# A hybrid decoder layer on one core: the recurrent gates' block products as two row tiles of 64

## The reference

```python
LRU_WIDTH = 512; LRU_BLOCKS = 8; LRU_BLOCK = 64

def rglru_group(u, gate_in, conv_w, conv_b, w_gate_a, b_gate_a, w_gate_x, b_gate_x, lru_lambda):
    xc = causal_conv_of_width_4(u) + conv_b
    xb = xc.reshape(B, T, LRU_BLOCKS, LRU_BLOCK)
    r = sigmoid(einsum("bthi,hij->bthj", xb, w_gate_a).reshape(B, T, C) + b_gate_a)
    i = sigmoid(einsum("bthi,hij->bthj", xb, w_gate_x).reshape(B, T, C) + b_gate_x)
    log_a = -8.0 * r * softplus(-lru_lambda)
    a, b = exp(log_a), sqrt(-expm1(2.0 * log_a)) * (i * xc)
    hseq = associative_scan(h[t] = a[t] * h[t - 1] + b[t])
    return hseq * gelu(gate_in)

# the layer
h   = x + RMSNorm( [ rglru_group ; diff_attn_group ] W_out )
out = h + RMSNorm( relu(RMSNorm(h) W_up)^2 W_down )
```

## Time and profile before

| | |
|---|---|
| time, median of 3 runs | 1154.75 us (1152.32 to 1155.97) |
| time of the profiled execution | 1152.76 us |
| span of the profiled execution, first to last instruction | 1151.0 us |
| busy TensorE, share of the span | 1122.8 us, 98% |
| busy VectorE | 785.3 us, 68% |
| busy ScalarE | 399.2 us, 35% |
| mean granted TensorE clock | 0.996 |

### The profile page before, as it was taken

How to read it: one execution, slowest core, us unless ns; L and a number is a source line. 1 busy time by engine, 2 the same in 40 slices (tenths; PEclk the granted TensorE clock), 3 DMA queues, 4 the chain that set the end, 5 groups by cost and what they waited for, 6 DMA issues and landing times.

```text
span 1151.0 us, 14008 instructions
## 1 busy us (share of the span) xinstructions
PE 1122.8 (98%) x5110; PEld 908.4 (79%) x5110; DVE 785.3 (68%) x1127; ACT 399.2 (35%) x728; POOL 52.7 (5%) x94
## 2 busy tenths in 40 slices
PE   7999999999989999999999999999999999999996
PEld 6888887777756788878888888888888888888885
DVE  6666765756577546888867667766766666766768
ACT  7433933545567326642212112212221211211222
POOL 0300001000121110000000000000000000000010
PEclk9999999999999999999999999999999999999998
DMA  6111323111010456111121011110211102111062
GB/s 229 56 37 36 136 84 89 58 37 38 21 35 19 148 182 200 73 37 74 37 73 36 36 73 36 45 64 36 73 36 41 69 36 73 36 36 73 37 234 113
DMA packets 23397, 83.11 MB, mean 72 GB/s; under 512 B 3088, under 2 KB 3216, under 8 KB 23232
## 3 DMA queue, kind: packets, MB, share of 16 engines
q1 hardware_dynamic: 17424, 62.92, 15.3%
q0 software_dynamic: 5648, 19.60, 5.0%
q10 hardware_dynamic: 288, 0.09, 0.0%
HBM read 70.02 MB, written 8.39 MB: 68 GB/s over the span
## 4 chain that ended last, share of the span: by engine, by line
PE 89%; DVE 5%; DMA 2%; ACT 1%; issue 1%; SPq 0%; POOL 0%; DVEq 0%; ACTq 0%
PE pair L352 27%; PE pair L354 27%; PE pair L353 27%; PE pair L725 3%; PE pair L760 2%; DMA raw<-weights 2%; PE pair L742 1%; PE pair L728 1%; DVE y_gain L2087 1%; PE pair L574 1%; DVE yacc L2072 1%; DMA q_rot<-q_sb 1%; DVE h_sb L2101 1%; DVE negmax L1657 0%; DVE wl L1478 0%
## 5 line engine op out<-in xcount | busy, mean ns | idle before, releaser
L354 PE MATMUL pair<-wdh,xl 128*128 128x512 f32 x480 | 186.7, 389 | 0.0
L352 PE MATMUL pair<-wdh,xh 128*128 128x512 f32 x480 | 186.7, 389 | 0.0
L353 PE MATMUL pair<-wdl,xh 128*128 128x512 f32 x480 | 186.7, 389 | 0.0
L1883 DVE TENSOR_TENSOR yacc<-yacc,pair 128x1024 f32<-128x1024 f32 x104 | 127.0, 1221 | 80.2 <-PE pair L354 80.2
L1378 ACT ACTIVATE up_h<-raw 128x384 fp32r<-128x384 f32 x56 | 27.4, 513 | 226.9 <-DMA raw<-weights 226.9
L353 PEld LDWEIGHTS pair<-wdl,xh 128*128 128x128 f32 x480 | 90.1, 188 | 18.7
L352 PEld LDWEIGHTS pair<-wdh,xh 128*128 128x128 f32 x480 | 90.1, 188 | 18.7
L354 PEld LDWEIGHTS pair<-wdh,xl 128*128 128x128 f32 x480 | 90.1, 188 | 18.7
L352 PE MATMUL pair<-xh,wh 128*128 128x512 f32 x256 | 102.2, 399 | 1.0 <-DVE xl L1501 1.0
L354 PE MATMUL pair<-xh,wl 128*128 128x512 f32 x256 | 99.9, 390 | 0.0
L353 PE MATMUL pair<-xl,wh 128*128 128x512 f32 x256 | 99.7, 389 | 0.0
(11 more groups left out here) (305 smaller groups left out, 2099.1 us busy)
## 6 DMA issues: line engine op xcount, KB each, us to landing
raw<-weights SPq DMA_DIRECT2D x74, 512.0 KB, 3.3
wd_f<-weights SPq DMA_DIRECT2D x28, 512.0 KB, 3.6
x_sb<-x SPq DMA_DIRECT2D x8, 512.0 KB, 7.7
q_rot<-q_sb POOLq DMA_DIRECT2D x32, 128.0 KB, 2.7
out<-h_sb POOLq DMA_DIRECT2D x8, 512.0 KB, 3.5
h_sb<-out POOLq DMA_DIRECT2D x8, 512.0 KB, 11.2
out<-h_sb SPq DMA_DIRECT2D x7, 512.0 KB, 2.6
x_a<-x POOLq DMA_DIRECT2D x4, 512.0 KB, 6.8
```

The lines of the kernel that those rows point to most:

```text
L352: pe.matmul(o, a_hi, b_hi, start=first, stop=False)
L353: pe.matmul(o, a_hi, b_lo, start=False, stop=False)
L354: return pe.matmul(o, a_lo, b_hi, start=False, stop=last)
L1883: dve.tensor_tensor(y, y, pair[2 + t % 2][:, :], ALU.add).then_inc(y_added, 1)
```

## The change

The two gates of one block go into one stationary tile. `gwh` and `gwl` hold 128x128 instead of 128x2x128 floats: rows 0 to 63 hold the first block's matrices, `a` in columns 0 to 63 and `x` in columns 64 to 127; rows 64 to 127 hold the second block's, `x` first. Each matmul now contracts over 64 rows. One with rows 0 to 63 writes `pair[2]` (gate `a` of block 1 on partitions 0 to 63, gate `x` on 64 to 127), the next with rows 64 to 127 writes `pair[3]` (gate `x` of block 2, then gate `a`). Their number stays 12, and the two row tiles alternate. ScalarE waits for all of them and applies four sigmoids of 64 partitions; for gate `x` it reads one half of the partitions and writes the other.

```diff
-        gwh = sb("gwh", [P, 2, P], F32R, at_s + 16 * KB)
-        gwl = sb("gwl", [P, 2, P], F32R, at_s + 17 * KB)
+        gwh = sb("gwh", [P, P], F32R, at_s + 16 * KB)
+        gwl = sb("gwl", [P, P], F32R, at_s + 17 * KB)
...
-        gw_raw = sb("gw_raw", [P, LC, 2, P], F32, at_v)
+        gw_raw = sb("gw_raw", [P, LC, P], F32, at_v)
...
             def gate_products(c):
                 pe.wait_ge(xc_lo, c + 1)
-                for g in range(2):
-                    for hf in range(2):
-                        tok = slice(HALF * hf, HALF * hf + HALF)
-                        mm = mm3(pe, pair[2 + g][:, tok], gwh[:, g, :], gwl[:, g, :], xch[:, tok],
-                                 xcl[:, tok], True, True)
-                    mm.then_inc(gates_done, 1)
+                for hf in range(2):
+                    tok = slice(HALF * hf, HALF * hf + HALF)
+                    for n, (w, u) in enumerate(((gwh, xch), (gwh, xcl), (gwl, xch))):
+                        for g, rows in enumerate((slice(0, 64), slice(64, P))):
+                            mm = pe.matmul(pair[2 + g][:, tok], w[rows, :], u[rows, tok], start=n == 0, stop=n == 2)
+                            if n == 2:
+                                mm.then_inc(gates_done, 1)
...
-                act.activation(gwh[:, :, :], gw_raw[:, c, :, :], ACT.Copy)
+                act.activation(gwh[:, :], gw_raw[:, c, :], ACT.Copy)
...
-                act.wait_ge(gates_done, 2 * c + 1)
-                act.activation(dec[:, c, :], pair[2][:, :], ACT.Sigmoid,
-                               bias=cols[:, bass.ds(c + C_BA, 1)]).then_inc(sig_done, 1)
-                act.wait_ge(gates_done, 2 * c + 2)
+                act.wait_ge(gates_done, 4 * c + 4)
+                act.activation(dec[0:64, c, :], pair[2][0:64, :], ACT.Sigmoid,
+                               bias=cols[0:64, bass.ds(c + C_BA, 1)]).then_inc(sig_done, 1)
+                act.activation(dec[64:P, c, :], pair[3][64:P, :], ACT.Sigmoid,
+                               bias=cols[64:P, bass.ds(c + C_BA, 1)]).then_inc(sig_done, 1)
                 act.wait_ge(ix_done, c)
-                act.activation(lru_a[:, :], pair[3][:, :], ACT.Sigmoid,
-                               bias=cols[:, bass.ds(c + C_BX, 1)]).then_inc(sig_done, 1)
+                act.activation(lru_a[0:64, :], pair[2][64:P, :], ACT.Sigmoid,
+                               bias=cols[0:64, bass.ds(c + C_BX, 1)]).then_inc(sig_done, 1)
+                act.activation(lru_a[64:P, :], pair[3][0:64, :], ACT.Sigmoid,
+                               bias=cols[64:P, bass.ds(c + C_BX, 1)]).then_inc(sig_done, 1)
...
-                dve.tensor_tensor(gwl[:, :, :], gw_raw[:, c, :, :], gwh[:, :, :].bitcast(F32), ALU.subtract)
+                dve.tensor_tensor(gwl[:, :], gw_raw[:, c, :], gwh[:, :].bitcast(F32), ALU.subtract)
...
-                dve.wait_ge(sig_done, 2 * c + 2)
+                dve.wait_ge(sig_done, 4 * c + 4)
```

More of the change, by code:

```diff
@@ L511, in _ @@
             pool.wait_ge(squares_v, 2)
-            pool.dma_start(gw_raw[:, :, :, :], gate_weights).then_inc(gates_loaded, 16)
+            pool.dma_start(gw_raw[:, :, :], gate_weights).then_inc(gates_loaded, 16)
             links = [0]
@@ L536, in _ @@
             nc.gpsimd.tensor_scalar(spl[:, 1, :], acc, -LRU_C, None, ALU.mult).then_inc(spl_ready, 1)
-            pool.wait_ge(gates_done, 2 * LC)
+            pool.wait_ge(gates_done, 4 * LC)
             pool.dma_start(cos_t[:, :, :], rope).then_inc(rope_loaded, 16)
@@ L672, in _ @@
                 else:
-                    pe.wait_ge(sig_done, 2 * LC)
+                    pe.wait_ge(sig_done, 4 * LC)
                 for j in range(N_V):
@@ L1117, in _ @@
                 hi(None, wh[1][:, :], (piece_used, 2 * c + 2, 1, 16 * c + 32))
-                act.wait_ge(gates_done, 2 * c + 1)
-                act.activation(dec[:, c, :], pair[2][:, :], ACT.Sigmoid,
-                               bias=cols[:, bass.ds(c + C_BA, 1)]).then_inc(sig_done, 1)
-                act.wait_ge(gates_done, 2 * c + 2)
+                act.wait_ge(gates_done, 4 * c + 4)
[3 more added lines that the diff above has]
+                               bias=cols[64:P, bass.ds(c + C_BA, 1)]).then_inc(sig_done, 1)
                 act.wait_ge(ix_done, c)
-                act.activation(lru_a[:, :], pair[3][:, :], ACT.Sigmoid,
-                               bias=cols[:, bass.ds(c + C_BX, 1)]).then_inc(sig_done, 1)
+                act.activation(lru_a[0:64, :], pair[2][64:P, :], ACT.Sigmoid,
+                               bias=cols[0:64, bass.ds(c + C_BX, 1)]).then_inc(sig_done, 1)
+                act.activation(lru_a[64:P, :], pair[3][0:64, :], ACT.Sigmoid,
+                               bias=cols[64:P, bass.ds(c + C_BX, 1)]).then_inc(sig_done, 1)
                 act.wait_ge(gelu_in, c + 1)
                 act.activation(lru_g[:, :], lru_g[:, :], ACT.Sigmoid, scale=GELU_S).then_inc(gelu_sig, 1)
-                act.wait_ge(sig_done, 2 * c + 2)
+                act.wait_ge(sig_done, 4 * c + 4)
                 if c == 0:
@@ L2150, in lay_out_gates @@
 def lay_out_gates(wa, wx):
[L2152 to L2156, removed]
+    g = np.empty((P, LC, P), np.float32)
+    for c in range(LC):
+        g[0:64, c, 0:64], g[0:64, c, 64:P] = wa[2 * c], wx[2 * c]
+        g[64:P, c, 0:64], g[64:P, c, 64:P] = wx[2 * c + 1], wa[2 * c + 1]
     return g
```

## The result

| | before | after |
|---|---|---|
| median of 10 runs | 1153.33 us (1151.85 to 1155.97) | 1157.08 us (1155.79 to 1159.29) |
| profiled execution, its span | 1152.76, 1151.0 | 1156.22, 1154.4 |
| mean granted clock | 0.996 | 0.994 |
| ratio of the medians | | 1.003 [1.0022, 1.0038] |

The change costs 2.5 to 4.4 us by the interval, 3.5 by the ratio and 3.75 by the medians: that it is slower is clear of noise, and its size lies on the line of 0.3% that the forecast drew. The time lies in the range. The forecast was +0.84 against its base, so the likeliest case had both waits in their places and came out some 3 us too low.

A forecast was written before the change was run, and what follows sets the result against it. TensorE, busy 98% of the span, was taken as the bound; 3.8 us gained in gate products would vanish in waits for ScalarE's sigmoids, leaving +0.84 at piece 10: 1153.6 profiled, 1155.6 us median. Range 1151.9 to 1158.3.

The forecast's parts named there:

- the line of 0.3%: Whole kernel: a measurement can tell a change from none at about 0.3%, 3.5 us.
- the likeliest case: Whole kernel: 0.84 us slower, 1155.6 us, without a fall of the clock; chance 0.42.
- both waits: New TensorE idle places: about 1.8 us before chunk 1's products, near 3 us before piece 10.
- A gate group on TensorE: Gate products of a chunk: paired row tiles take 1.76 us instead of 2.72, 0.96 us less.
- The rival without overlap: Gate products: row tiles do not run together, 3.1 us a group, 1158.3 us in all; chance 0.08.
- The sigmoids: ScalarE: four half sigmoids at full price, 1.0 us apart, take 2.0 us more per chunk.
- the rival of the dear crossings: Sigmoids crossing partitions in chunks 0 and 3: at twice the price, +4.8 us, 1159.6; chance 0.07.
- The cheap halves: ScalarE sigmoids: half the partitions cost half the time, 1151.9 us, 0.25% faster; chance 0.08.
- Piece 10: Behind chunk 3's sigmoids: `wh`, `wl` and piece 10 come +0.84 us; TensorE waits near 3.0 us.
- Chunk 1: First gate products: TensorE waits 1.8 us for `xcl`, starts +0.96 us and leaves 0.2 us ahead.
- The clock: Behind the new 3.0 us wait: 3.4 us at half speed may lose 1.7 us, +2.5, 1157.3; chance 0.28.
- Within 0.3%: Whole kernel: time stays within 0.3% of before; chance 0.82.

The follow-up runs named there:

- both waits filled: The change plus 8 needless TensorE products before chunk 1's gate products and 13 before piece 10: 1155.32 us against 1153.5, ratio 1.0016.
- the single filler: The change plus 12 needless TensorE products in the wait before piece 10 only: 1159.8 us, ratio 1.005; run again 1157.79 us, ratio 1.0037.

## Why the prediction came out as it did

*A gate group on TensorE*, 0.96 us less: right, 0.94 measured, and two tiles of fp32r products do run together. The rival without overlap is out. One detail failed: for chunk 1, whose products start out of a wait, I charged the way in to the wait altogether and let the group end after 1.36 + 0.20. The change's timeline of TensorE, behind the wait and ahead of chunk 3's products:

```profile
66.30 0.40 PE L625 MATMUL pair<-xcl,gwh 64*128 64x512 f32 x2
...
67.55 0.50 PE L352 MATMUL pair<-xh,wh 128*128 128x512 f32 x1
67.88 0.40 PE L353 MATMUL pair<-xl,wh 128*128 128x512 f32 x1
...
112.81 0.39 PE L354 MATMUL pair<-xh,wl 128*128 128x512 f32 x1
113.13 0.50 PE L625 MATMUL pair<-xch,gwh 64*128 64x512 f32 x2
```

The first pair pays for its weights even after a wait (66.30 - 65.97 = 0.33). The group leaves at 67.55 against 67.70, what follows is dear once more (67.88 - 67.55 = 0.33), so the shift behind it is -0.05 and not -0.2, and at 89.24 both kernels stand level. Chunk 2 adds its 0.94, of which 0.91 are there before chunk 3's products (112.81 against 113.72), and the way in takes 0.09 of it: -0.81, where -1.16 was forecast.

*The sigmoids*, 2.0 us per chunk: **the term that was mis-sized**; it is 2.54. The step "I take the full price: the 1024 columns are the same" was right for the duration and wrong for what counts, the distance of the starts. 1.00 between two full sigmoids contained an overlap of 0.1 us which the split takes away: the start-to-start time of like neighbours was carried over to unlike ones. The Trainium skill, ScalarE: Activation LUTs (What ACT_TABLE_LOAD costs), has back-to-back ACTIVATEs overlap by about 93 ns. The rows agree for neighbours that begin on the same partition (1.11 - 1.02 = 0.09 and 1.12 - 1.01 = 0.11) and disagree for those that don't. The bound "twice the price" was the rival of the dear crossings; halves that don't cross cost the same 1.14, so it is out as a mechanism, and as a size it was far off. The cheap halves are out as well, since a half takes 1.01.

*Piece 10*, +0.84: +1.59. Of the difference of 0.75, 0.54 are the sigmoids of chunk 3. Another 0.24 were missing ahead of them, since they start at 116.50 against 117.42, 0.92 early and not 1.16; and 0.03 go the other way. The path was the forecast one: TensorE's gain ends in a wait for `wl`, 3.25 us where near 3.0 were expected. *Chunk 1*: wait 1.85 (1.8), start +0.99 (+0.96). That this came out so near, although its sigmoids were sized too low, is in part luck. VectorE's step behind them was 2.06 us late (54.05 against 51.99) where +1.76 was forecast; only 0.12 of those 0.30 us were left at `xcl` (64.69 against 63.05, +1.64 for +1.52).

*The clock.* Here the choice failed. The likeliest branch was that the granted clock would not fall, 0.42 against 0.28, although the text had the wait of 3.0 us "longer than those two together". What spoke against a fall was read rightly: the kernel before kept 1.00 also behind its wait of 1.97 us, from 192.3 to 200. It just said little of a wait of 3 us. The clock fell in both profiles of the change, and from 129.13 to 195.41 are 66.28 us where before had 64.79, 1.5 more (1.7 forecast); with both waits filled it is gone. With the fall the forecast was +2.5; the 0.75 of piece 10 on top give +3.25 against 3.4 of span measured.

So the number given for the likeliest case was too low by a sigmoid overlap and a clock fall. Two things about the hit are luck. The time is inside the range whose top, 1158.3, came from the case without overlap (+3.56), which did not occur: two other terms came to the same size. And the base was lower than assumed, 1153.33 and not 1154.75; on the assumed base +3.5 to +3.75 would have been 1158.2 to 1158.5, on that top. "Within 0.3%", given 0.82, is not a clean hit either: the ratio is 1.0030 and the medians are 0.33% apart.

*Still open.* Why the single filler gave 6.1 us more by its medians at first and 4.9 the second time was not settled. The clock fell at 67.2 and 196.9 us in the one profile and at 195.2 in the other, but a profile shows one execution, and behind waits near 1.85 us it fell in some of them only. The mean granted clock of all its runs was 0.992 against 0.994 in before the first time and 0.993 against 0.995 the second. By estimate (0.0020 and 0.0016 of 1155 us) that is 2.3 and 1.8 us, and the version with both waits filled, which lost no clock, was 1.8 us slower; that leaves 2.0 and 1.3 us without a cause.

## What to carry to other kernels

A gain on the bounding engine is worth what the queue that feeds its next wait allows: tile where the feeding engines have room (three of four groups gained 2.7 us here, by the ratio), and leave it where they don't. Before splitting an elementwise step into halves, price each half at a whole entry without overlap, since columns and first partitions count and the number of partitions doesn't. A new TensorE wait of 2.5 us or more next to dense work should be priced with a fall of the clock: behind all five such waits here it was at one half for 3.4 us or more.

## What the runs showed of the hardware

- ScalarE takes the same time for 64 partitions as for 128 (1024 columns: 1.01 and 1.00 us from start to start). If the first partition read or written (the bias goes with it) changes between two neighbours, it is 1.12 to 1.15. A half by columns (512) is 0.57.
- Row tiles of 64 cost about 0.09 us of waiting and 0.10 us of uncovered weight load on the way in, and the same on the way out, 0.4 us a visit; between these a pair costs 0.23 us like one full product.
- Between 60 and 200 us the granted clock fell to one half behind every wait of TensorE that was longer than 2 us: 2.51, 2.77, 3.24 and twice 3.25. Behind shorter ones it fell in some profiles and not in others, and the length doesn't tell which. Before chunk 1 it fell behind 1.84 and 1.87 us, but not behind 1.83, 1.84 (twice) and 1.85. Before the first scores it fell behind 1.66, 1.78 and 1.91, but not behind nine others, of 1.54 to 1.97. It stayed down for 3.4 or 6.8 us; where the change had the shorter fall, it lost 1.5 to 1.6 us by it.
